# Norm sums with tokens on partitions, and roots of 5 columns spread back over partitions by TensorE

## The reference

```python
def rms_norm(x, g):
    y = x32 * lax.rsqrt(jnp.mean(x32 * x32, axis=-1, keepdims=True) + EPS)
    return (y * g.astype(jnp.float32)).astype(x.dtype)
...
    h = modulate(rms_norm(x, norm1_g), sh1, sc1)
    z = h @ w_in
...
    hc, new_buf = causal_depthwise_conv(hc, conv_buf, conv_w, conv_b)
    hc = jax.nn.silu(layer_norm(hc, conv_ln_g, conv_ln_b))
    hs, hT_re, hT_im = s5_mixer(u, h0_re, h0_im, ...)
    mix = jnp.concatenate([hc, hs.astype(hc.dtype)], axis=-1) @ w_out
    x = x + g1[:, None, :] * mix
    h2 = modulate(rms_norm(x, norm2_g), sh2, sc2)
    x = x + g2[:, None, :] * peer_ffn(h2, peer_w_q, peer_keys, peer_u, peer_v)
...
        y = modulate(rms_norm(x, final_norm_g), shift, scale)
```

## Time and profile before

| | |
|---|---|
| median of 3 runs | 1766.14 us (1764.98 to 1767.88) |
| span of the profiled execution | 1764.8 us |
| TensorE busy | 1706.6 us, 97% |
| VectorE busy | 1137.4 us, 64% |
| ScalarE busy | 671.5 us, 38% |
| GpSimd busy | 813.4 us, 46% |
| share of TensorE in the chain that ended last | 92% |
| DVE reciprocal of 520 columns (L1112), 3 times | 3.40 us each |
| mean granted TensorE clock | 0.988 of full |

### The profile page before, as it was taken

One profiled execution on the slowest core, in us unless ns is written; L12 is line 12 of the kernel. 1 busy time (PEld: TensorE's weight loads), 2 busy tenths in 40 slices (PEclk: granted clock), 3 DMA queues, 4 the chain that ended last, 5 costly groups with the idle time before them and its releaser, 6 DMA issues.

```text
span 1764.8 us, 33989 instructions
## 1 busy us (share of the span) xinstructions
PE 1706.6 (97%) x13543; PEld 1567.5 (89%) x13543; DVE 1137.4 (64%) x3012; ACT 671.5 (38%) x1220; POOL 813.4 (46%) x683
## 2 busy tenths in 40 slices
PE   5999988999999999999999999999999999999996
PEld 2885687899999999999999999998888888888885
DVE  8989834199993766666666660166666666666655
ACT  2323333333333444444444443343333333333334
POOL 1200022345545333333333444467777777777730
PEclk8999999999999999999999999999999999999999
DMA  8555543568888788888888888599999999999971
GB/s 306 127 157 183 134 122 130 181 186 239 239 246 232 217 243 254 246 253 253 250 236 246 254 257 260 195 329 339 382 390 377 379 363 355 380 378 368 371 277 54
DMA packets 307709, 458.51 MB, mean 260 GB/s; under 512 B 27008, under 2 KB 217648, under 8 KB 305504
## 3 DMA queue, kind: packets, MB, share of 16 engines
q1 hardware_dynamic: 273648, 355.86, 64.2%
q0 software_dynamic: 33904, 100.48, 16.0%
HBM read 396.27 MB, written 127.10 MB: 297 GB/s over the span
## 4 chain that ended last, share of the span: by engine, by line
PE 92%; DVE 4%; ACT 2%; DMA 1%; issue 1%; POOL 0%; SPq 0%; DVEq 0%; ACTq 0%
PE ps L1981 42%; PE ps L2016 26%; PE ps L1680 8%; PE ps L1960 5%; PE ps L1970 4%; PE ps L1634 1%; PE ps L1877 1%; DVE rstd L1112 1%; PE ps L1928 1%; PE ps L1768 0%; DMA raw<-in_v 0%; PE ps L1652 0%; PE ps L1819 0%; PE ps L1848 0%; DMA act_spill<-actr 0%
## 5 line engine op out<-in xcount | busy, mean ns | idle before, releaser
L1981 PE MATMUL ps<-h,hl 128*128 128x256 f32 (+1 forms) x6144 | 812.9, 287 | 0.0
L1981 PEld LDWEIGHTS ps<-h,hl 128*128 128x128 f32 x6144 | 758.6, 189 | 0.1
L866 ACT ACTIVATE hl<-raw 128x512 fp32r<-128x512 f32 x512 | 322.3, 630 | 683.6 <-PE ps L1981 468.2
L637 POOL TENSOR_TENSOR hl<-raw,hl 128x512 fp32r<-128x512 f32 x260 | 357.1, 1376 | 471.0 <-ACT hl L866 470.7
L2016 PEld LDWEIGHTS ps<-WH,hl 128*128 128x128 f32 x3072 | 472.5, 188 | 40.4 <-issue 38.6
L2016 PE MATMUL ps<-WH,hl 128*128 128x336 f32 x3072 | 487.0, 318 | 1.3 <-ACT actr L899 1.3
L1564 DVE TENSOR_TENSOR hl<-raw,hl 128x512 fp32r<-128x512 f32 x252 | 175.1, 696 | 206.7 <-ACT hl L866 205.6
L645 POOL DMA_INDIRECT gathered_act<-act_spill,act_index x184 | 207.1, 1125 | 62.2 <-issue 55.7
L654 POOL DMA_INDIRECT v_rows_ring<-v_rows,v_row_index x184 | 196.3, 1067 | 74.3 <-issue 53.1
L1493 DVE TENSOR_SCALAR ohA<-ps,selT 128x128 f32<-128x128 f32 x336 | 117.3, 349 | 163.1 <-PE ps L1970 151.4
L1494 DVE TENSOR_SCALAR ohB<-ps,selT 128x128 f32<-128x128 f32 x336 | 135.1, 402 | 0.0
(11 more groups left out here) (306 smaller groups left out, 1282.9 us busy)
## 6 DMA issues: line engine op xcount, KB each, us to landing
raw<-in_u SPq DMA_DIRECT2D x128, 512.0 KB, 6.7
v_rows<-in_v SPq DMA_DIRECT2D x128, 512.0 KB, 6.1
raw<-in_v SPq DMA_DIRECT2D x128, 512.0 KB, 8.6
act_spill<-actr SPq DMA_DIRECT2D x128, 260.0 KB, 2.9
raw<-in_w_ada SPq DMA_DIRECT2D x64, 512.0 KB, 4.4
gate_spill<-stage SPq DMA_DIRECT2D x21, 1024.0 KB, 7.5
hring<-act_spill SPq DMA_DIRECT2D x128, 168.0 KB, 6.6
gbp<-gate_spill SPq DMA_DIRECT2D x16, 1344.0 KB, 8.9
```

What stands on the lines that cost most here:

```text
L637: pool.tensor_tensor(hl[:, n % 2, 1, c], raw[:, n % NRAW, c], hl[:, n % 2, 0, c].bitcast(F32), ALU.subtract).then_inc(s_wlo, 1)
L866: act.activation(hl[:, n % 2, 0, c], raw[:, n % NRAW, c], ACT.Copy).then_inc(s_whi, 1)
L1981: last = pe.matmul(ps[:, 2 * (m % 2) + h, 0:b - a], hl[:, m % 2, w, q * P:(q + 1) * P], h2[:, r, q, a:b], start=q == 0 and (w, r) == (0, 0 ...
```

## The change

The operands of the sums change places. The squares of up to 128 tokens are now the stationary operand and one column of ones is moved, so each of 5 products (128, 8, 128, 128 and 128 tokens, in the order in which they are issued) leaves its tokens' sums in one column of PSUM, a token on each partition. Additions, reciprocal and root work on `token_stats` [128 x 5]. TensorE then spreads the roots: each column, repeated over 128 columns as stationary operand, times the identity gives that chunk's roots on every partition, in one bank of PSUM (512 prompt tokens) and 8 columns of another (samples). VectorE reads them from there instead of `rstd`. The gathered tokens' norm keeps its form. Cut to its core:

```diff
+        tstat = sb(base, "token_stats", [P, 8])
...
+        TOK = tuple((P * c, min(P * c + P, T)) for c in range(-(-T // P)))
+
+        STAT_BANKS = {"rms1": (2, 3), "conv": (4, 5), "rms2": (4, 5), "final": (4, 5)}
+
+        def root_of(norm):
+
+            wide, narrow = STAT_BANKS[norm]
+            return ps[:, wide, 0:TP], ps[:, narrow, P:P + TS]
+
...
             def root(norm):
                 act.wait_ge(s_rec, RSTD[norm])
-                act.activation(rstd[:], rstd[:], ACT.Sqrt).then_inc(s_rstd, 1)
+                act.activation(tstat[:, 0:5], tstat[:, 0:5], ACT.Sqrt).then_inc(s_rstd, 1)
...
-            def reciprocals(norm, width):
+            def reciprocals(norm, width, tokens=T):
+
                 dve.wait_ge(s_stat, STAT[norm])
-                for h, (a, b) in enumerate(HALVES):
-                    last = dve.tensor_scalar(rstd[:, a:b], ps[:, 4 + h, 0:b - a], 1.0 / width, EPS, ALU.mult, ALU.add)
+                bank, full = STAT_BANKS[norm][1], tokens // P
+                if full:
+                    last = dve.tensor_scalar(tstat[:, 0:full], ps[:, bank, 0:full], 1.0 / width, EPS, ALU.mult, ALU.add)
+                if tokens % P:
+                    rows = slice(0, tokens - P * full)
+                    last = dve.tensor_scalar(tstat[rows, full:full + 1], ps[rows, bank, full:full + 1], 1.0 / width, EPS,
+                                             ALU.mult, ALU.add)
                 link(last)
-                dve.reciprocal(rstd[:], rstd[:]).then_inc(s_rec, 1)
...
+                dve.reciprocal(tstat[:, 0:5], tstat[:, 0:5]).then_inc(s_rec, 1)
...
-                    dve.scalar_tensor_tensor(dst[:, q, 0:TP], x[:, q, 0:TP], gsc[:, i, q, 0:1], rstd[:, 0:TP],
+                    dve.scalar_tensor_tensor(dst[:, q, 0:TP], x[:, q, 0:TP], gsc[:, i, q, 0:1], wide,
...
-            dve.wait_ge(s_rstd, RSTD["rms1"])
+            dve.wait_ge(s_rb, RSTD["rms1"])
...
                 dve.tensor_tensor(mixin[:, t, 0:TP].rearrange("p (i c) -> p i c", i=L), natural(cv[:, t, 0:TP]),
-                                  natural(rstd[:, 0:TP]), ALU.mult)
-                dve.tensor_tensor(mixin[:, t, TP:T], cv[:, t, TP:T], rstd[:, TP:T], ALU.mult).then_inc(s_cn, 1)
+                                  natural(wide), ALU.mult)
+                dve.tensor_tensor(mixin[:, t, TP:T], cv[:, t, TP:T], narrow, ALU.mult).then_inc(s_cn, 1)
...
-                for h, (a, b) in enumerate(HALVES):
-                    last = pe.matmul(ps[:, 4 + h, 0:b - a], ones[:], sq[:, q % 2, a:b], start=q == 0, stop=q == KD - 1)
-                last.then_inc(s_squ if q < KD - 1 else s_stat, 1)
+                token_sums(norm, q, KD)
+
+            def token_sums(norm, q, count, tokens=T):
+
+                chunks = [(c, a, min(b, tokens)) for c, (a, b) in enumerate(TOK) if a < tokens]
+                chunks.insert(1, chunks.pop())
+                for c, a, b in chunks:
+                    last = pe.matmul(ps[0:b - a, STAT_BANKS[norm][1], c:c + 1], sq[:, q % 2, a:b], ones[:, 0:1],
+                                     start=q == 0 and c == 0, stop=q == count - 1 and (c, a, b) == chunks[-1])
+                last.then_inc(s_squ if q < count - 1 else s_stat, 1)
+
+            def spread_roots(norm, tokens=T):
+
+                pe.wait_ge(s_rstd, RSTD[norm])
+                wide, narrow = STAT_BANKS[norm]
+                for c, (a, b) in enumerate(TOK):
+                    if a < tokens:
+                        n = min(b, tokens) - a
+                        dst = ps[:, wide, a:a + n] if a < TP else ps[:, narrow, P:P + n]
+                        last = pe.matmul(dst, tstat[0:n, c:c + 1].broadcast_to([n, P]), ident[0:n, 0:n],
+                                         start=c == 0 or a == TP, stop=a == TP or a + n == min(TP, tokens))
+                last.then_inc(s_rb, 1)
...
+                            if kind == "out" and tile == 0 and i == 1:
+                                spread_roots("conv")
...
-            modulation_rows(0, 6, KD)
+            modulation_rows(0, 6, 7)
+            spread_roots("rms1")
+            modulation_rows(0, 7, KD)
...
-            modulation_rows(3, 0, 2)
+            modulation_rows(3, 0, 1)
+            spread_roots("rms2")
+            modulation_rows(3, 1, 2)
...
             for q in range(4, KD):
                 final_sums(q)
+            spread_roots("final", ND)
```

More of the change, by code:

```diff
@@ L290, in build @@
         s_rec = sem("reciprocal_ready")
-        s_rstd = sem("rstd_ready")
+        s_rstd = sem("token_root_ready")
+        s_rb = sem("roots_spread_over_partitions")
         s_hs = sem("normed_scaled")
@@ L720, in gathered_root @@
                 act.wait_ge(s_frc, 1)
-                act.activation(rstd[:, ND:T], rstd[:, ND:T], ACT.Sqrt).then_inc(s_frs, 1)
+                act.activation(rstd[:], rstd[:], ACT.Sqrt).then_inc(s_frs, 1)
             def gathered_shifts():
@@ L969, in _ @@
             final_squares(KD - 1)
-            act.wait_ge(s_rec, RSTD["final"])
-            act.activation(rstd[:, 0:ND], rstd[:, 0:ND], ACT.Sqrt).then_inc(s_rstd, 1)
+            root("final")
             for k in range(KD):
@@ L1323, in _ @@
             reciprocals("conv", CC)
-            dve.wait_ge(s_rstd, RSTD["conv"])
+            dve.wait_ge(s_rb, RSTD["conv"])
+            wide, narrow = root_of("conv")
             for t in range(CT):
                 dve.tensor_tensor(mixin[:, t, 0:TP].rearrange("p (i c) -> p i c", i=L), natural(cv[:, t, 0:TP]),
-                                  natural(rstd[:, 0:TP]), ALU.mult)
-                dve.tensor_tensor(mixin[:, t, TP:T], cv[:, t, TP:T], rstd[:, TP:T], ALU.mult).then_inc(s_cn, 1)
+                                  natural(wide), ALU.mult)
+                dve.tensor_tensor(mixin[:, t, TP:T], cv[:, t, TP:T], narrow, ALU.mult).then_inc(s_cn, 1)
                 if t:
@@ L1354, in _ @@
             gain(1, SC2)
-            variance("rms2", D)
+            reciprocals("rms2", D)
+            dve.wait_ge(s_rb, RSTD["rms2"])
             dve.wait_ge(s_os, 16 * (CT + 3))
@@ L1576, in gathered_reciprocals @@
                 dve.wait_ge(s_fst, 1)
-                link(dve.tensor_scalar(rstd[:, ND:T], ps[:, 6, 0:NG], 1.0 / D, EPS, ALU.mult, ALU.add))
-                dve.reciprocal(rstd[:, ND:T], rstd[:, ND:T]).then_inc(s_frc, 1)
+                link(dve.tensor_scalar(rstd[:], ps[:, 6, 0:NG], 1.0 / D, EPS, ALU.mult, ALU.add))
+                dve.reciprocal(rstd[:], rstd[:]).then_inc(s_frc, 1)
             def gathered_apply():
                 dve.wait_ge(s_frs, 1)
-                r = rstd[:, TP:T].rearrange("p (o s) -> p o s", o=1).broadcast_to([P, KD, TS])
+                r = rstd[:, TP - ND:NG].rearrange("p (o s) -> p o s", o=1).broadcast_to([P, KD, TS])
                 tt(smalls[:], x[:, :, TP:T], r, ALU.mult)
@@ L1610, in _ @@
             add_out(NK - 1)
-            dve.wait_ge(s_stat, STAT["final"])
-            link(dve.tensor_scalar(rstd[:, 0:ND], ps[:, 4, 0:ND], 1.0 / D, EPS, ALU.mult, ALU.add))
-            dve.reciprocal(rstd[:, 0:ND], rstd[:, 0:ND]).then_inc(s_rec, 1)
-            dve.wait_ge(s_rstd, RSTD["final"])
+            reciprocals("final", D, ND)
+            dve.wait_ge(s_rb, RSTD["final"])
             for q in range(KD):
-                dve.scalar_tensor_tensor(yo[:, q, 0:ND], x[:, q, 0:ND], gsc[:, 2, q, 0:1], rstd[:, 0:ND],
+                dve.scalar_tensor_tensor(yo[:, q, 0:ND], x[:, q, 0:ND], gsc[:, 2, q, 0:1], root_of("final")[0][:, 0:ND],
                                          ALU.mult, ALU.mult).then_inc(s_hs, 1)
@@ L1901, in _ @@
             modulation_rows(2, 7, KD)
-            column_sums(sq_rows, CT, lambda q: (s_sq, SQ_BEFORE["conv"] + q + 1), True)
+            for q in range(CT):
+                pe.wait_ge(s_sq, SQ_BEFORE["conv"] + q + 1)
+                token_sums("conv", q, CT)
             pe.wait_ge(s_gsig, CT)
@@ L1999, in final_sums @@
                 pe.wait_ge(s_sq, SQ_BEFORE["final"] + q + 1)
-                pe.matmul(ps[:, 4, 0:ND], ones[:], sq[:, q % 2, 0:ND], start=q == 0, stop=q == KD - 1)\
-                    .then_inc(s_squ if q < KD - 1 else s_stat, 1)
+                token_sums("final", q, KD, ND)
             pe.wait_ge(s_act, NTT + NK)
```

11 lines of the change are left out of this document (5 added, 6 removed).

## The result

| | before | after |
|---|---|---|
| median of 4 runs each, side by side | 1765.83 us | 1773.9 us (1772.82 to 1778.35) |
| span of the profiled execution | 1764.8 us | 1772.7 us |
| mean granted TensorE clock | 0.988 | 0.980 |

The ratio is 1.0047, 95% interval 1.0035 to 1.0059: the changed kernel is 8 us **slower**, where 10.7 us less (1755.4) was forecast.

A forecast was written before the change was run, and what follows sets the result against it. TensorE, busy all but 4.5 us in the expert and second products, was taken to pass earlier gains on to the end. 1.8 + 2.6 + 1.7 + 2.0 + 1.3 + 1.3 = 10.7 off 1766.1 gave 1755.4 us, range 1752.5 to 1762.5.

The forecast's parts named there:

- First norm: In the first norm, modulations start 1.8 us earlier; dearer sums are hidden by 3 us of cover before VectorE's additions.
- Rival 2: One-column products let the clock fall during the sums, so conv products start at half clock: 1761.0 us, chance 0.13.
- Rival 3: Loads are not hidden behind one-column products, each record costs 190 ns, and the kernel is slower: 1767.5 us, chance 0.08.
- The clock terms: Behind the conv and second norms, TensorE's idle time shrinks and the clock stays full: 1.7 and 1.3 us gained.
- additions, reciprocal, root: In the norms, this small step on at most 5 columns takes 0.9 us, 0.7 at the lower end.
- sums of a tile, full clock: A channel tile's ten records on TensorE take 0.98 us against 0.88, so 0.10 more.
- spreading, full clock: Four 128x128 products and one of 8 columns, which VectorE waits for, take 1.2 us.
- spreading in the last norm: In the last norm, spreading the roots takes 3 products and 0.95 us.
- last norm as a whole: The last norm gains 1.3 us: 3.35 becomes 0.9 + 0.95, and five sums cost 0.04 each.
- join of the stages: Time gained before the join between the stages is passed on to the kernel's end.
- Reading from PSUM: VectorE's reading of the roots from PSUM, strided in the conv norm, was taken to cost no change.
- Rival 4: The join's wait for a load of v absorbs earlier gains, only the last norm's 1.3 stays: 1764.8 us, chance 0.07.

The follow-up runs named there:

- e9: Changed kernel with only the first norm in the new form, 96 moved columns instead of one, other norms as before: 1767.98 us, ratio 1.0015.
- e2: Changed kernel with only the first norm in the new form, one moved column, other three norms as before: 1773.25 us, ratio 1.0045.
- e10: Changed kernel with its first norm as before, one moved column in the other three: 1764.92 us, ratio 0.9993.
- e6: Changed kernel with its first norm as before, 96 moved columns instead of one in the other three: 1763.08 us, ratio 0.9981.
- e8: Changed kernel with only the last norm in the new form, one moved column, other three as before: 1765.59 us, ratio 0.9994.
- e5: Kernel before plus unread identity products ahead of four u tiles: 20 and 60 moving one column, 60 moving 32, 60 moving 96; the sixty one-column products took 23.51 us.
- e11: Changed kernel with its first norm as before, 64 moved columns instead of one in the other three: 1763.12 us, ratio 0.9981.

## Why the prediction was wrong

**The step that failed** is in "First norm": "the sums end at 31.38: 3 us of cover for 8 x 0.10". It went wrong twice. The price was that of the full clock. One record cost 0.10 us at full clock (second norm) and 0.197 at half; the first norm begins at half, and with the one-column products the clock did not come up until about 44 us. With 96 columns in the same place (e9: same loads, same number of records) it rose between 26 and 27 us, and the modulations were added at 45.08 instead of 49.17. And the cover was measured to VectorE's additions, the wrong partner. The sums share TensorE's queue with the modulation rows, and each weight load is issued only when a row has freed its place, so a delay of the sums is passed on to the loads: they were issued over 18.18 us instead of 9.77. The sums ended at 39.40 instead of 31.38, far beyond the 3 us of cover, and even then the chain ran over the loads and not over VectorE. Forecast - 1.8, measured + 6.3. e2 shows it alone, e10 shows it gone.

**Rival 2** ("One-column products leave the array idle enough that the clock falls") named the cause: the clock falls behind such products, though what in the array makes it fall is not shown. It had 0.13 and a price of 5.6 us of lost gain (4.3 + 1.3), since it was worked out only where a fall was in view, in the conv norm and the second norm. That the rise in the first norm hangs on the same thing was not seen. With it the rival's 1761.0 would have been 1761.0 + 1.8 + 6.3 = 1769.1, on the other side of no change.

**Rival 3** (each load 190 ns) is refuted: ten records take 1.00 us at full clock, 0.100 each, with a load each. The Trainium skill, page "TensorE: Matmul & The Clock Gate", section "Part 3: Packing small matmuls — row/col tiling", has loads overlap running products only in other row groups; the estimate made with that page's figures was 1.16 us a tile. The measurement decides: 1.00, all loads full height.

**The clock terms (1.7 and 1.3).** "With them, I expect, goes the half clock" took idle time for the only cause. After, TensorE is busy without a gap from 220 to 231 us and the clock falls from 1.00 to 0.50 all the same, behind the sums. The half clock has been given a new cause, and moved onto the spreading and the first products. e6 shows what the terms were worth with a full clock. Its conv norm takes 2.3 us less than before's, and 1.5 less than the mean of the six old forms (195.56), where 4.3 was forecast. From the additions to the first multiplication it is 2.24 us instead of 4.90, close to the forecast gain of 2.8. But the additions start at 219.58 instead of 217.83: the forty records of the sums take 5.53 us where sixteen took 3.89, and all of them stand ahead of the additions, for which the prediction had counted 0.2 (with one column 4.59 in after, so 0.7). The first multiplication comes 0.9 earlier (221.82 against 222.73). Behind the last low part, where the clock is now full, the products take 3.93 us instead of 5.29: 1.4 of the forecast 1.7.

**The other terms, by what they measured:**

| term | forecast | measured |
|---|---|---|
| additions, reciprocal, root | 0.9 us (0.7 lower end) | 0.7 in the chain of the last norm (1762.35 to 1763.05) |
| sums of a tile, full clock | 0.98 | 1.00 in the second norm, 1.13 in the conv norm |
| sums of a tile, half clock | not priced | 1.97 |
| spreading, full clock | 1.2 | 1.41 to 1.48 (with 96 columns); 2.24 to 2.54 where the clock was at half |
| spreading in the last norm | 0.95 | 0.91 after; 1.58 at half in e8 |
| last norm as a whole | - 1.3 | - 0.2 after, - 1.0 in e8 and e10, - 1.4 with 96 columns |
| join of the stages | passes all on | + 5.95 us before it (1169.68 to 1175.63), kept |

Reading from PSUM costs nothing, as forecast: eight readings in the second norm take 5.35 us against 5.38 before, and four with a stride in the conv norm 1.09 to 1.17 each against 1.07 to 1.19. Rival 4, the join that absorbs, did not happen: the difference that arrives is passed on, and 2.08 us join it, 1.1 of them at the join, where the store of `act_spill` took longer. Why it did is not shown, and the same code varies by 3.3 us.

## What to carry to other kernels

Ask for each product what it does to TensorE's clock, not only what it lasts: a long row of products with few moved columns was dear here by what ran beside and behind it, and dearest at the place where the clock still had to rise. Price a step in TensorE's queue against everyone who waits for that queue, loads that wait for a freed buffer included. If a narrow form is wanted, put it only where the clock is full already, and pad its moved operand: here the first took away 9 us and the second another 1.8, so that + 8 us became - 3.4.

## What the hardware showed

- The granted clock falls with TensorE busy all the time. In e5, with identical loads back to back, it falls to 0.50 with 1 and with 32 moved columns and stays 1.00 with 96; within the three later norms it is 1.00 with 64 too (e11). The Trainium skill, page "TensorE: Matmul & The Clock Gate", section "What's actually happening", says that the clock is set by how busy TensorE has been recently. The trace agrees only if that is not the busy time which the profile counts: the `448.00:455.00` window is busy for all of its 7.00 us, at 0.50.
- What a product's record costs with more columns differs by place: 0.109 us with one column (e5, twenty products, full clock), 0.111 with 96 (13.37 us for 120 records). In the second norm it is 0.100 with one column, 0.119 with 64 and 0.129 with 96. So 96 columns cost 2% more than one in e5 and 29% more there. Why the two differ was not tested.
- Loads of full height overlap with products: two load records of 190 ns each and the one-column products between them pass in 0.20 us at full clock (second norm).
- The same instructions take different times where they wait for transfers, and the same time where they do not: from the first key product to the join 825.12 to 825.13 us in all thirteen executions, from the first key product to the last block of `v` ahead of the last norm 1390.58 to 1393.90 us. So an effect of 2 us behind the join says nothing in one trace of this kernel.
